# Squared-ReLU layers: high and low parts of the activation behind each other in one 512-column matmul, with the halves of the bank added by GpSimd

## The reference

```python
def sq_relu_mlp(h, w_in, w_out):          # h 256 x 1024, w_in 1024 x 4096, w_out 4096 x 1024
    a = jax.nn.relu(h @ w_in)
    return (a * a) @ w_out

# in first_block, for i in range(2):
    h = rms_norm(x, mlp_norm[i])
    x = x + sq_relu_mlp(h, mlp_w_in[i], mlp_w_out[i])
```

## Time and profile before

| | |
|---|---|
| median of 3 runs | 1002.38 us (1001.0 to 1002.65) |
| profiled execution, its own time | 1002.42 us |
| its span in the trace | 1000.6 us |
| PE busy | 965.4 us (96%) |
| PEld busy | 828.2 us (83%) |
| DVE busy | 682.0 us (68%) |
| ACT busy | 518.0 us (52%) |
| POOL busy | 53.3 us (5%) |
| granted TensorE clock, mean | 0.994 |

### The profile page before, as it was taken

One profiled execution on the slowest core, in us unless ns is written; L12 is line 12 of the kernel. 1 busy time (PEld: TensorE's weight loads), 2 busy tenths in 40 slices (PEclk: granted clock), 3 DMA queues, 4 the chain that ended last, 5 costly groups with the idle time before them and its releaser, 6 DMA issues. The chain is left out here.

```text
span 1000.6 us, 14873 instructions
## 1 busy us (share of the span) xinstructions
PE 965.4 (96%) x5844; PEld 828.2 (83%) x5844; DVE 682.0 (68%) x948; ACT 518.0 (52%) x715; POOL 53.3 (5%) x71
## 2 busy tenths in 40 slices
PE   7989999999999999999999999999988989999997
PEld 5468889988978877899999887889866789999996
DVE  2676658999755666647788665467565687777775
ACT  2565665445446665554545554454566454444443
POOL 0310000000001110000001000000011000000000
PEclk9999999999999999999999999999997999999999
DMA  9132666767655732677988562232210535555541
GB/s 355 75 127 84 228 236 226 276 228 275 249 204 195 236 126 93 218 283 287 336 301 328 176 252 76 94 126 85 84 43 10 199 124 222 184 182 179 182 169 43
DMA packets 29520, 185.06 MB, mean 185 GB/s; under 512 B 3616, under 2 KB 4320, under 8 KB 10016
## 3 DMA queue, kind: packets, MB, share of 16 engines
q1 hardware_dynamic: 24192, 155.54, 42.8%
q0 software_dynamic: 4416, 28.31, 7.7%
q10 hardware_dynamic: 864, 0.55, 0.2%
HBM read 181.77 MB, written 2.62 MB: 184 GB/s over the span
## 5 line engine op out<-in xcount | busy, mean ns | idle before, releaser
L2027 DVE TENSOR_TENSOR split<-raw,split 128x2048 fp32r<-128x2048 f32 x122 | 279.6, 2292 | 178.5 <-ACT split L1467 177.0
L1467 ACT ACTIVATE split<-raw 128x2048 fp32r<-128x2048 f32 x121 | 231.5, 1913 | 233.5 <-PE bank L732 219.9
L730 PE MATMUL bank<-acts,split 128*128 128x256 f32 (+1 forms) x960 | 278.1, 290 | 2.7 <-DVE acts L2067 1.4
L731 PE MATMUL bank<-acts,split 128*128 128x256 f32 (+1 forms) x960 | 276.7, 288 | 0.0
L732 PE MATMUL bank<-acts,split 128*128 128x256 f32 (+1 forms) x960 | 276.7, 288 | 0.0
L730 PE MATMUL bank<-split,acts 128*128 128x512 f32 (+1 forms) x544 | 211.6, 389 | 2.7 <-DVE acts L2709 1.3
L731 PE MATMUL bank<-split,acts 128*128 128x512 f32 (+1 forms) x544 | 208.7, 384 | 0.0
L732 PE MATMUL bank<-split,acts 128*128 128x512 f32 (+1 forms) x544 | 208.6, 383 | 0.0
L730 PEld LDWEIGHTS bank<-acts,split 128*128 128x128 f32 x960 | 183.7, 191 | 9.9 <-DVE split L2027 3.3
L731 PEld LDWEIGHTS bank<-acts,split 128*128 128x128 f32 x960 | 183.8, 191 | 3.5
L732 PEld LDWEIGHTS bank<-acts,split 128*128 128x128 f32 x960 | 183.8, 191 | 1.9
(11 more groups left out here) (251 smaller groups left out, 1022.8 us busy)
## 6 DMA issues: line engine op xcount, KB each, us to landing
raw<-w_mlp SPq DMA_DIRECT2D x64, 1024.0 KB, 4.8
raw<-w_glu SPq DMA_DIRECT2D x22, 1024.0 KB, 4.8
bias<-w_ada POOLq DMA_DIRECT2D x14, 1024.0 KB, 6.8
raw<-w_qkv SPq DMA_DIRECT2D x12, 1024.0 KB, 5.5
arena<-w_glu_down SPq DMA_DIRECT2D x22, 512.0 KB, 3.3
work<-w_ada POOLq DMA_DIRECT2D x10, 1024.0 KB, 6.2
raw<-w_mla_o SPq DMA_DIRECT2D x4, 1024.0 KB, 5.1
raw<-w_moba_o SPq DMA_DIRECT2D x4, 1024.0 KB, 4.7
```

Of the source, the lines that this page charges most:

```text
L730: pe.matmul(out_, a[0], b[0], start=first, stop=False)
L731: pe.matmul(out_, a[0], b[1], start=False, stop=False)
L1467: return act.activation(out_, in_, ACT.Copy)
L2027: v.tensor_tensor(split[:, c % 2, 1, 0:n], raw[:, c % 2, 0:n], split[:, c % 2, 0, 0:n].bitcast(F32), ALU.subtract).then_inc(lo_ready, 1)
```

## The change

An up unit now makes its two halves in two banks. The high and the low part of the activation, which lie behind each other in `acts`, pass in one matmul of 512 columns against the high weights: high x high falls into columns 0 to 255, high x low into columns 256 to 511. Low weights x high activation stays a matmul of 256 columns, into columns 0 to 255. The two halves of a bank must then be added. ACT copies each bank to SBUF (`both_t`), GpSimd adds the halves (128x256, two to an up unit), and ReLU reads the sum from SBUF. On DVE, the low part of the hidden features (`hidden`) moves behind the modulation work of its chunk. The loads of `w_ada` on POOL's queue now stand behind the adds of a certain up unit.

```diff
@@ the table of the gemms: name, chunks, units, group @@
-("mlp0", 32, 16, 1)
+("mlp0", 32, 32, 1)
-("mlp1", 32, 16, 1)
+("mlp1", 32, 32, 1)
@@ TensorE @@
+            def wide_products(u, w, n, ks=range(KD)):
+                bank = gbank(u + n)
+                for k in ks:
+                    w_hi, w_lo = (p[:, k, n * P:(n + 1) * P] for p in w)
+                    both, hi = acts[:, 0, :, k * T:(k + 1) * T], acts[:, 0, 0, k * T:(k + 1) * T]
+                    if k < KD - 1:
+                        pe.matmul(bank[:, :], w_hi, both, start=k == 0, stop=False)
+                        pe.matmul(bank[:, 0:T], w_lo, hi, start=False, stop=False)
+                    else:
+                        pe.matmul(bank[:, 0:T], w_lo, hi, start=False, stop=False)
+                        pe.matmul(bank[:, :], w_hi, both, start=False, stop=True).then_inc(gemm_ready, 1)
+            def wide_unit(c, u, i=None):
+                w = slot(c, KD, 256)
+                for n in range(2):
+                    gemm_start(u + n, i, 2)
+                    wide_products(u, w, n)
@@ ScalarE @@
+            def halves_out(name, s, f, i=None):
+                u = GU[name] + 2 * s + f
+                gemm_out(act, u, i, 8)
+                copy(both_t[:, f], gbank(u)[:, :].rearrange("p (a b) -> p a b", a=2)).then_inc(gemm_free[u % 4], 1)
                 def chunk(n, i=None):
+                    if not seq[n][0]:
+                        halves_out(name, seq[n][1], 0, i)
                     used(c0 + n, i, 8)
                     if not seq[n][0]:
                         hidden(seq[n][1], i)
...
                 def hidden(s, i=None):
-                    u = GU[name] + s
-                    act.activation(relu_t[:, s % 2, :], gbank(u)[:, :], ACT.Relu).then_inc(gemm_free[u % 4], 1)
-                    act.wait_ge(gemm_free[u % 4], u // 4 + 1 if i is None else i + (u // 4 + 1))
+                    halves_out(name, s, 1, i)
+                    n = 2 * s + 2 + SUM0[name]
+                    act.wait_ge(up_summed, n if i is None else 8 * i + n)
+                    act.activation(relu_t[:, s % 2, :], relu_t[:, s % 2, :], ACT.Relu).then_inc(rectified, 1)
+                    act.wait_ge(rectified, HID0[name] + s + 1 if i is None else 4 * i + (HID0[name] + s + 1))
@@ GpSimd @@
+            def halves_added(name, s, dst):
+                for f in range(2):
+                    u = GU[name] + 2 * s + f
+                    gemm_gone(pool, u)
+                    pool.tensor_tensor(dst[:, f, :], both_t[:, f, 0, :], both_t[:, f, 1, :], ALU.add).then_inc(up_summed, 1)
+            def mlp(name, layer, first, last, land, after):
+                due = {j: ada_done(layer, j - 2) for j in range(first + 2, last)}
+                for s in range(16):
+                    halves_added(name, s, relu_t[:, s % 2, :].rearrange("p (a b) -> p a b", a=2))
...
+                    for j, n in due.items():
+                        if n in (2 * s - 2, 2 * s - 1):
+                            pool.wait_ge(ada_used, j - 1)
+                            ada_load(j, land)
@@ VectorE, mlp @@
                     used(c0 + n)
+                    if n < 2 * steps - 3:
+                        beside(n)
                     if not seq[n][0]:
                         hidden(seq[n][1])
-                    beside(n)
+                    if n >= 2 * steps - 3:
+                        beside(n)
```

More of the change, by code:

```diff
@@ L103, in plan @@
                 if not is_down:
-                    released.append(("gemm", unit + step + 1))
+                    released.append(("gemm", unit + 2 * (step + 1)))
                 elif step < n // 2 - 1:
@@ L165, with ada_done @@
 HID0 = dict(mlp0=0, mlp1=16, glu=32)
+SUM0 = dict(mlp0=0, mlp1=32)
+def ada_done(layer, j):
+    return max(n for n, items in ADA[layer].items() if any(x[0] == j for x in items))
 RAW = ("h0", "m0", "h1", "m1")
@@ L319, in program @@
         square_t = view(arena, 1024, 2, 512)
+        both_t = view(arena, 9216, 2, 2, T)
         ctx = view(work, 0, 2, D)
@@ L440, in sbank, with gemm_out @@
             return ps[4 + u % 4]
-        def gemm_out(eng, u, i=None):
-            eng.wait_ge(gemm_ready, u + 1 if i is None else 4 * i + (u + 1))
+        def gemm_out(eng, u, i=None, per=4):
+            eng.wait_ge(gemm_ready, u + 1 if i is None else per * i + (u + 1))
         def gemm_gone(eng, u):
@@ L660, in _ @@
             roots(3, 7)
[L662 to L668, removed]
+            def mlp(name, layer, first, last, land, after):
+                due = {j: ada_done(layer, j - 2) for j in range(first + 2, last)}
+                for s in range(16):
+                    halves_added(name, s, relu_t[:, s % 2, :].rearrange("p (a b) -> p a b", a=2))
+                    if s == 1:
+                        pool.wait_ge(act_lo, LO0[name] + 1)
+                        for j in range(first, first + 2):
+                            ada_load(j, land)
+                        roots(after[0], after[0] + 1)
+                    for j, n in due.items():
+                        if n in (2 * s - 2, 2 * s - 1):
+                            pool.wait_ge(ada_used, j - 1)
+                            ada_load(j, land)
+                    if s == 11:
+                        roots(*after[1])
+            mlp("mlp0", 0, 0, 10, att, (7, (8, 8)))
             for m in range(2):
@@ L691, in _ @@
             roots(10, 11)
[L693 to L700, removed]
+            mlp("mlp1", 1, 10, 24, bias, (11, (12, 13)))
+            roots(13, 14)
             pool.memset(cumr[:, :].bitcast(F32), 0.0).then_inc(zeros_ready, 1)
@@ L808, in cols_unit, with first_up_wide @@
                 ins.then_inc(gemm_ready, 1)
+            def wide_products(u, w, n, ks=range(KD)):
[14 more added lines that the diff above has]
+                    wide_products(u, w, n)
+            def first_up_wide(c, u, name, tiles=4, units=2):
+                w = slot(c, KD, 256)
+                for n in range(2):
+                    gemm_start(u + n)
+                for k0 in range(0, KD, tiles):
+                    pe.wait_ge(act_lo, LO[name] - 4 + units * (k0 // tiles + 1))
+                    for n in range(2):
+                        wide_products(u, w, n, range(k0, k0 + tiles))
             def first_up(c, u, name, tiles=4, units=2):
@@ L830, in up @@
                     if n == 0:
-                        first_up(c0, u0, norm)
+                        first_up_wide(c0, u0, norm)
                     else:
-                        cols_unit(c0 + n, u0 + s, (0, 1), (0, 0), i)
+                        wide_unit(c0 + n, u0 + 2 * s, i)
                 def down(n, s, i=None):
@@ L1477, in used @@
             def used(c, i=None, pitch=0):
-                per = {"gemm": 4, "down": pitch // 2}.get(RELEASED[c][0], 0)
+                per = {"gemm": 8 if pitch == 8 else 4, "down": pitch // 2}.get(RELEASED[c][0], 0)
                 released(act, c, i, per)
```

9 lines of the change are left out of this document (5 added, 4 removed).

## The result

The kernel with the change takes 1032.27 us (median; 1027.2 to 1034.1) against 1002.32 us for the kernel before on the same chip (1001.0 to 1002.65): a ratio of 1.0293, 95% interval 1.0253 to 1.0333, or about 29 us. The forecast was 1015 us, range 1001 to 1032. It is slower, as forecast, but by well over twice as much. The profiled execution took 1033.61 us, with a span of 1031.8.

A forecast was written before the change was run, and what follows sets the result against it. The prediction took PE to set the pace, with DVE almost full in the first layer. Matmul gain, ordinary pairs, first down chunks and indicator pairs, -6.0 + 7.3 + 4.0 + 7.0 = +12.3 us on 1002.42, gave 1015 us, range 1001 to 1032.

The forecast's parts named there:

- What bounds the kernel: Both changed layers: PE sets the pace, but in the first DVE, 89.47 us of 100 busy, has almost nothing left.
- The first down chunks: First down chunk of each layer: PE stalls 1.9 us plus 0.1 for the restart, in two layers +4.0 us.
- the ordinary pairs: Pairs of down chunk and up unit without indicator: PE stalls 0.33 us in each of 22, +7.3 us.
- the indicator pairs: Eight pairs with an indicator on DVE: 12.0 us against PE's 11.03, 0.88 more for each, +7.0 us.
- POOL is passed over: Rival, adds on POOL: they also wait out DVE's next operation, 1.14 us later; +18 on top, 1032 us; 15 in 100.
- I take 0 and keep 4 for the range: `w_ada` loads behind the adds: data arrive about when DVE asks; 0 to 4 us in the second layer, 0 taken.
- 6.0 us for 32 units: Up units on PE: two of three 256-column matmuls become one of 512, saving 0.187 us a unit.
- The rival's bound: Up units on PE: the gain could fall to 0; rival "PE gains nothing, or the loads are late", 1019 to 1021, 10 in 100.

The follow-up runs named there:

- short loads: The change with all `w_ada` loads but the first two of a layer cut to 128 of 2048 columns: 1.0195 of the kernel before.
- the copies alone: The change with ACT copying both banks but POOL adding nothing, ReLU reading the copies' first halves: 0.9994 of the kernel before.
- slow writes: The change with POOL's adds replaced by memsets, one for the first bank, six for the second: 1.0143 of the kernel before; with short loads 1.0109.
- later features: The change with ReLU, Square and both feature parts mostly moved behind the following down chunk's weight split: 1.0214 of the kernel before.
- the memsets: The change with POOL's two adds of a unit replaced by two memsets of the same tile, all waits kept: 1.0045 of the kernel before.

## Why the prediction was off in size

The direction was right, and so was most of the working. The experiments make a ladder from the kernel before to the change:

| step | timed | from | in the two layers of the traces | forecast |
|---|---|---|---|---|
| wide matmuls, with the copies | -0.6 us (-0.9 and +0.2 without the copies) | 0.9994 | -1.9 | -6.0 |
| chain split, add, ReLU in ACT's queue, with the first down chunks | +11.5 | 1.0109 - 0.9994 | +9.1 | 7.3 + 4.0 + 7.0 for this row and the next two |
| DVE held by the adds | +6.9 | 1.0108 - 1.0039 | +3.9 | in the row above |
| chain and hold together | +1.7 | 1.0195 - 1.0109 - 0.0069 | +8.2 | in the row above |
| `w_ada` loads | +9.1 | 1.0286 - 1.0195 | +7.6 | 0 |
| sum | +28.6 | | +26.8 | +12.3 |

Each timed difference carries 3 to 4 us of uncertainty, the fourth row 5. The traces are one execution each, and two of the change differ by 2 us in each layer. A layer counts here from its first up unit to its last.

The table has no row of its own for the granted clock, for which the forecast has no term either. Its mean is 0.991 in the eight timed executions of the change, 0.994 in those with short loads and 0.995 in those of the kernel before, in which 0.001 less goes with some 0.8 us more. By that estimate the clock makes about 3 of the change's 29 us. In the traces of the change and of the kernel with short loads 3.4 us are two falls in the first layer, part of the fourth row.

- **What bounds the kernel**: held. Where DVE has next to nothing left, the eight pairs with indicators grew from 91.2 to 103.2 us in all, most of the 15.0 us that the first layer lost. Those behind a large indicator take 13.7 to 14.2 us where they took 11.5, the others 11.2 to 12.7 where they took 11.3.
- **The first down chunks, the ordinary pairs, the indicator pairs**: held, if the terms are laid beside the kernel that has chain and hold but not the loads' bytes (the change with short loads, its trace against that of the copies alone). The first down chunks cost 3.9 us, forecast 4.0. The 18 ordinary pairs between first and last up unit cost 5.2, 0.29 each, forecast 0.33; they don't repeat, some stall 1 to 2 us and others nothing. The indicator pairs cost 12.0, or 8.6 without the two falls of the clock, forecast 7.0.
- **But not by the chain alone.** With slow writes and short loads the ordinary pairs cost 0.09 each. That the timed 11.5 of the second row looks like 7.3 + 4.0, and the 6.9 of the third like 7.0, is luck: 4.1 us of the chain lie in the indicator pairs, and the hold makes the chain dearer there. That an add holds DVE is seen directly (1.22 to 1.76 us).
- **"POOL is passed over"**, the rival at 1032 us, came out near the time but for a wrong reason. The adds end 0.58 to 0.61 us behind the end of a DVE operation also where the next one follows without a gap.
- **The step that failed first: "I take 0 and keep 4 for the range"** for the `w_ada` loads. It asked only whether the modulation data reach DVE in time. DVE indeed waits 2.7 us for them. The cost is to the other queue: at 0.83 of the DMA time in use the weight loads had just enough time, and the late splits, which the working itself had found, took that time from them. The cost is 9 us timed, 7.6 of them seen in the layers; it is 3.9 with the loads' place alone, where DVE waits 16.6 us for modulation data as well, and 3.4 with the slow writes' chain.
- **The term that was mis-sized: "6.0 us for 32 units"**. The trace of the change has 3.8, since 0.352 us pass where 0.348 were assumed. The kernel with nothing else of the change has 2.6 in its layers and, timed, a gain of 0.9 and a loss of 0.2, neither clear of zero. Why the 3.8 don't show in the time stays open. The rival's bound ("the gain could fall to 0") was the value to take.

No kernel here beats the one before, and since the part that was to bring the gain is no faster by itself, no mended version promised to.

## What to carry to other kernels

Before work is moved to GpSimd because it is idle, count the two-operand DVE operations around it: here an add of 128x256 that met one waited for it to end, and then took some 0.54 us from the next one if that followed at once, so it was paid for on DVE although POOL was only 17% busy. When a step makes the operations late that free a load's slot, redo the sum of the loads at once, with all queues that share the DMA engines; here the loads cost nearly as much as the chain itself. A gain of 12 ns for each pair of matmuls made into one should be run by itself first.

## What the hardware showed that was not expected

The granted clock fell to half for 3.4 us twice in the first layer of the change, at 205.4 and 256.6 us. Windows of the first (columns as in the earlier trace rows):

```profile
204.00:205.50 1.50, 1.19 (x6) 0.99 (x7) 1.50 (x4) 0.27 (x1) 0.00 (x0) 0.92 0.65 142
205.50:208.50 3.00, 3.00 (x12) 2.61 (x11) 3.00 (x3) 0.00 (x0) 0.00 (x0) 0.50 0.81 314
208.50:210.00 1.50, 1.50 (x9) 1.32 (x9) 1.47 (x3) 0.60 (x1) 0.34 (x1) 0.94 0.43 76
```

0.50 is the 1.2 GHz level. Just ahead PE had waited 2.06 us for DVE's split, as it had ahead of the second:

```profile
204.31 0.50 PE L837 MATMUL bank<-acts,split 128*128 128x512 f32 x1 [2.06 <-DVE split L2087]
...
205.63 0.63 PE L837 MATMUL bank<-acts,split 128*128 128x512 f32 x1
206.06 0.41 PE L838 MATMUL bank<-acts,split 128*128 128x256 f32 x1
206.28 0.63 PE L837 MATMUL bank<-acts,split 128*128 128x512 f32 x1
```

The starts are 0.43 and 0.22 apart instead of 0.23 and 0.12, so a fall costs 1.7 us. Both falls begin about 1 us into an up unit that had waited. Other stalls were followed by none, for instance that of 1.69 us at the layer's first down chunk, and in the second run of the change the falls came at other places (230 and 582 us). In the first layer the trace has one or two falls for the change and for every kernel that keeps its waits for adds (short loads, later features, DVE's order as before, loads between the adds), and none for the others: before, the wide matmuls, the copies, the memsets, slow ones too, and the adds that nobody waits for. So the falls look like a price of the stalls, paid on top of them; no run here tests it by itself.
